# Last units of w_out by column halves over both token halves, and the first token half's transposes behind one unit more

## The chip, the cores and the metric

One Trainium2 chip, one core. The metric is the device time of the kernel in microseconds (us). The core has TensorE (matmuls), VectorE, ScalarE, GpSimd and SyncE (SP, which issues nearly all transfers here), and 16 DMA engines that bring the weights from memory.

## What is computed

A hybrid encoder layer on 256 tokens of width 1024: an RMS norm, a wide projection, a gated linear attention branch and a Hyena branch, their gated sum `merged`, the output projection `w_out`, and then a mixture of 32 experts of which each token takes 4. The part that matters here is the end of the mixer and the start of the experts:

```python
merged = jax.nn.sigmoid(g_gla) * (o_gla @ w_branch_gla) + jax.nn.sigmoid(g_hy) * (o_hy @ w_branch_hy)
h = h + merged @ w_out
hn = rms_norm(h, norm2_w)
h = h + moe_ffn(hn, router_w, router_b, w_gate_up, b_gate_up, w_down, b_down)
...
logits = ht.astype(jnp.float32) @ router_w.astype(jnp.float32) + router_b.astype(jnp.float32)
top_vals, top_idx = lax.top_k(logits, TOP_K)
```

All of it is float32. The weights of the 32 experts are about 400 MB and are read once.

## The kernel before

**The front.** Weights come in chunks of 1 MB through four front slots of the ring, two units to a chunk. Each unit is split by ScalarE and VectorE into a high and a low part ("parts"), and TensorE makes three passes per block of 128 rows. `w_out` has eight units: four units (two blocks of rows each) for each of two column halves. With the 256 tokens in two halves there are four PSUM banks, named `wo` + column half + token half: `wo00`, `wo01`, `wo10`, `wo11`. One unit for one token half is six matmuls of 128x512. Units 0 and 1 of both column halves run first for both token halves; units 2 and 3 are the last units. Step ("wo", half, a) runs both last units of one bank, twelve matmuls; ("wo_part", u) runs one of them for `wo11`, six matmuls.

**The list of stages.** `schedule()` writes out one list. TensorE, ScalarE and VectorE each walk through the whole list in order and do their own share of each stage, so the list fixes the order on each of the three engines; an engine waits on semaphores where it needs another's result. The tail of the list is on lines 263 to 265. What each step is:

- `wo`, `wo_part`: TensorE's matmuls (line 881); VectorE adds the finished bank to the residual `x` (line 1957).
- `hT` a n: four TensorE transposes of token half a, column half n of `x` (line 846); VectorE multiplies the bank by the norm's weight into `hT` (line 2005).
- `ss2` a: ScalarE's sum of squares and root of token half a (lines 1391 and 1456); `rs2`: VectorE's reciprocal (line 1972).
- `hn` a: ScalarE's high part of the normed token half (line 1460), then VectorE's low part (line 1739).
- `rl` a: the router product (TensorE, line 1123), then VectorE's logits, top-4 and mask (lines 1981 to 1989). `rank` a: the ranks of the chosen tokens (TensorE lines 1135 and 1136, VectorE lines 1993 and 1733).
- `total` 0 starts the output accumulation (line 955), `bias0` loads the biases of expert 0 (line 962). Then come the gathers (lines 947 and 939) and the experts (line 1161 gate and up, 1179 down).

**The loads.** SP issues the expert weights in a fixed order into a ring of 18 slots (and two places aside). Behind `w_out` the loads of chunks 12 to 15 each wait until a front chunk has been used (line 791): chunk 14 waits for bank `wo01`, chunk 15 for `wo11`. Later loads wait until TensorE has used the chunk that held the slot (`chunks_used`, line 807, by `uses_before`, line 169): chunk 20 waits for the first chunk of expert 0; chunks 6 and 7 lie aside and free no slot, and chunk 26, the load issued at 346.53 us, waits for chunk 8, the first of expert 1.

Of the kernel before, what the change touches and what calls it, by code (L numbers as in the profile page):

```python
# [223 lines left out]
def schedule():  # L224

    hyena = [("proj", k, 4 * half + b) for half in range(2) for k in ("hv", "hx") for b in range(4)]
    hyena += [("proj", "h0", b) for b in range(DB)]

    def tok(kind, half, units=range(4)):
        return [("tok", kind, half, u) for u in units]

    v0, v1 = tok("v", 0), tok("v", 1)
    st = [("xT", n) for n in range(4)] + v0[:1] + [("wa_parts",), ("filter", 1)] + v0[1:] + [("a_low",), ("filter", 2)]
    st += v1[:1] + [("gates", 0), ("gates", 1)] + v1[1:2] + [("gates", 2), ("gates", 3)]
    st += v1[2:3] + [("decay", 0)] + v1[3:] + [("decay", 1)]
    st += [("proj", "q", 0), ("proj", "q", 1)] + [("taps", 0, c) for c in TAP_ORDER] + [("proj", "q", 2), ("softplus",)]
    st += [("taps", 1, c) for c in TAP_ORDER] + [("proj", "q", 3), ("proj", "k", 0), ("sums", 0), ("proj", "k", 1), ("energy",)]
    st += [("proj", "k", 2), ("square", 0), ("proj", "k", 3)]  # L240
    rest = [[("energy_rest", 3 * h + i - 6)] if 2 <= h and 3 * h + i < 11 else [] for h in range(HEADS) for i in range(3)]
    for h in range(HEADS):
        st += [("scores", h)] + hyena[6 * h:6 * h + 2] + ([] if h else [("square", 1)]) + rest[3 * h]
        st += [("output", h)] + ([("sums", h + 1)] if h + 1 < HEADS else [])
        st += hyena[6 * h + 2:6 * h + 4] + rest[3 * h + 1] + hyena[6 * h + 4:6 * h + 6] + rest[3 * h + 2]
    st += [("ksum",), ("onorm",)] + [("zt", a, half) for half in range(2) for a in range(TB)]
    st += [("K", ri, half) for ri in range(2) for half in range(2)] + [("Z", half) for half in range(2)]
    r0, r1 = tok("r", 0), tok("r", 1)
    gg0, wg0, gg1 = tok("gg", 0), tok("wg", 0), tok("gg", 1)

    def Z(half, *steps):
        return [("Zmul", half, k) for k in steps]

    st += r0[:1] + Z(0, 0, 1) + r0[1:2] + Z(0, 2, 3) + r0[2:3] + Z(0, 4, 5) + r0[3:]
    st += r1[:1] + Z(0, 6) + [("silu", 0)] + r1[1:2] + Z(0, 7) + r1[2:3] + Z(1, 0) + r1[3:] + [("silu", 1), ("gated",)]
    st += gg0[:2] + [("oT", n) for n in range(4)] + gg0[2:4] + Z(1, 1)
    for u in range(4):
        st += wg0[u:u + 1] + Z(1, 2 + u) + [("zbias", u)]
    st += gg1[:1] + Z(1, 6) + gg1[1:2] + Z(1, 7) + gg1[2:]
    st += [("y", b) for b in range(DB)] + tok("wg", 1) + [("ohy_parts",)] + tok("gh", 0) + [("bias_parts",)] + tok("wh", 0)  # L260
    st += tok("gh", 1) + [("mT", 0), ("mT", 1)] + tok("wh", 1)
    st += tok("wo", 0, (0, 1)) + tok("wo", 1, (0,)) + [("mT", 2), ("mT", 3)] + tok("wo", 1, (1,))
    st += [("prepare",), ("wo", 0, 0), ("wo", 1, 0), ("ss2", 0), ("wo", 0, 1), ("hT", 0, 0), ("hT", 0, 1), ("rs2", 0), ("hn", 0)]
    st += [("wo_part", 2), ("rl", 0), ("hT", 1, 0), ("wo_part", 3), ("ss2", 1), ("total", 0), ("hT", 1, 1), ("rs2", 1)]
    st += [("rank", 0), ("rl", 1), ("bias0",), ("hn", 1), ("rank", 1)]

    def last_use(j):
        kind, nm, at, *u = UNITS[j]
        if nm == "wo" and u[0] > 1:
            return st.index(("wo_part", 3) if at else ("wo", 0, 1))  # L270
        return st.index(UNITS[j])

    for j in range(len(UNITS)):
        after = [st.index(("xT", min(j, 4) - 1)) if j else -1]
        if j // UNITS_PER_CHUNK >= FSLOTS:
            after.append(last_use((j // UNITS_PER_CHUNK - FSLOTS + 1) * UNITS_PER_CHUNK - 1))
        if j >= HI_BUFS:
            after.append(last_use(j - HI_BUFS))
        if j:
            after.append(st.index(("parts", j - 1)))  # L280
        st.insert(max(after) + 1, ("parts", j))
    return st


STAGES = schedule()
assert [s for s in STAGES if s in UNITS] == [u for u in UNITS if u[1] != "wo" or u[3] < 2]

# [1853 lines left out]
```

## Time and profile before

| | |
|---|---|
| median of 3 runs | 1248.22 us (1247.18 to 1248.77) |
| profiled run, its own time | 1248.36 us |
| span of the profiled run | 1246.6 us |
| mean granted TensorE clock | 0.998 |
| TensorE busy | 1166.2 us (94%) |
| VectorE busy | 416.2 us (33%) |
| ScalarE busy | 267.9 us (21%) |
| chain that ended last | TensorE 71%, DMA 22%, VectorE 4%, ScalarE 2% |

The span runs from the first to the last instruction; 1.8 us of the profiled run's time lie around it. Times in the rows below are from the start of the span. A busy share is a mean over stages with different limits; what the change touches lies between 304 and 320 us.

### The profile page before, as it was taken

To read this page: it belongs to the slowest core of one execution; us is meant where nothing else is said; L and a number is where in the kernel's file an instruction comes from. 1 tells how busy PE (TensorE), PEld (TensorE's weight loads), DVE (VectorE), ACT (ScalarE), POOL (GpSimd) and SP (SyncE) were. 2 spreads that over 40 slices of the span, in tenths; PEclk is the share of its full clock that TensorE was granted. 3 is DMA by queue.
4 is the path that set the end of the run, shared out by engine and by line. 5 is a ranking of instruction groups with operands and counts; after the bars stand their busy time and mean duration, and the time that the engine had idled before them with its cause. 6 is when DMAs were issued, how large, how long until landed. Compare 5 with 4: busy or idle time off the path is not lost.

```text
span 1246.6 us, 13718 instructions
## 1 busy us (share of the span) xinstructions
PE 1166.2 (94%) x5828; PEld 598.0 (48%) x5828; DVE 416.2 (33%) x702; ACT 267.9 (21%) x420; POOL 0.2 (0%) x4
## 2 busy tenths in 40 slices
PE   7999999999999999999999999988998899889986
PEld 6899968888533333343333334333433333233332
DVE  7677878756421122121212121211221121111212
ACT  6966546444200000010010001000100000001002
POOL 0000000000000000000000000000000000000000
PEclk9999999999999999999999999999999999999999
DMA  9455425698999999999999999999999999999995
GB/s 323 140 146 159 144 94 171 235 382 309 360 375 430 428 426 427 428 428 428 427 427 428 427 427 427 428 428 428 428 427 428 427 428 427 428 426 428 427 425 225
DMA packets 66941, 455.20 MB, mean 365 GB/s; under 512 B 6874, under 2 KB 23547, under 8 KB 39614
## 3 DMA queue, kind: packets, MB, share of 16 engines
q1 hardware_dynamic: 65302, 454.00, 89.1%
q8 instruction: 48, 0.79, 0.3%
q10 hardware_dynamic: 1576, 0.29, 0.1%
q14 instruction: 15, 0.12, 0.0%
HBM read 453.22 MB, written 1.05 MB: 364 GB/s over the span
## 4 chain that ended last, share of the span: by engine, by line
PE 71%; DMA 22%; DVE 4%; ACT 2%; issue 1%; SPq 0%; DVEq 0%; ACTq 0%
PE bank L1161 23%; DMA ring<-in_w_gate_up 18%; PE bank L1179 14%; PE total L881 6%; PE bank L881 4%; PE total L869 4%; PE bank L869 3%; DMA ring<-in_w_down 3%; PE bank L939 2%; PE bank L1147 2%; PE bank L1168 1%; PE total L1161 1%; ACT xn_area L1618 1%; PE bank L962 1%; PE total L1190 1%
## 5 line engine op out<-in xcount | busy, mean ns | idle before, releaser
L1161 PE MATMUL bank<-ring,hy_area 128*64 128x512 f32 x1984 | 441.8, 596 | 21.9 <-DMA ring<-in_w_gate_up 21.7
L1161 PEld LDWEIGHTS bank<-ring,hy_area 128*64 128x64 f32 x1984 | 135.6, 137 | 298.7 <-issue 251.5
L1179 PE MATMUL bank<-ring,xn_area 128*64 128x512 f32 x992 | 220.1, 595 | 20.6 <-ACT xn_area L1618 20.3
L1179 PEld LDWEIGHTS bank<-ring,xn_area 128*64 128x64 f32 x992 | 68.4, 137 | 150.6 <-issue 122.8
L2039 DVE TENSOR_SCALAR qk_area<-bank 128x512 f32<-128x512 f32 x31 | 21.5, 692 | 342.9 <-PE bank L1161 342.9
L2050 DVE SCALAR_TENSOR_TENSOR xn_area_r<-bank,tmp_area,xn_area_r 128x512 fp32r<-128x512 f32 x31 | 23.3, 751 | 307.0 <-ACT xn_area_r L1625 307.0
L1614 ACT ACTIVATE qk_area<-qk_area 128x512 f32<-128x512 f32 x32 | 20.2, 631 | 461.3 <-DVE qk_area L2039 461.3
L1747 DVE TENSOR_TENSOR front_r<-ring,slot_r 128x1024 fp32r<-128x1024 f32 x60 | 73.2, 1222 | 24.2 <-ACT slot_r L1426 24.1
L1426 ACT CAST slot_r<-ring 128x1024 fp32r<-128x1024 f32 x60 | 62.8, 1049 | 43.1 <-PE bank L881 23.2
L1625 ACT ACTIVATE xn_area_r<-bank,tmp_area 128x512 fp32r<-128x512 f32 x31 | 21.3, 687 | 229.1 <-PE bank L1179 212.0
L962 PE MATMUL bank<-tmp_area_r 128*128 128x512 f32 x124 | 36.9, 419 | 13.5 <-issue 8.5
L881 PE MATMUL total<-front_r,slot_r 128*128 128x512 f32 x112 | 43.6, 389 | 0.0
L1190 PE MATMUL total<-xn_area_r 64*128 64x512 f32 x248 | 37.2, 418 | 0.0
L1147 PE MATMUL bank<-tmp_area,tab 64*128 64x256 f32 x128 | 36.1, 402 | 0.7 <-ACT xn_area L1618 0.7
L2012 DVE TENSOR_SCALAR hy_area<-bank,colw 128x256 f32<-128x256 f32 x32 | 14.0, 478 | 66.3 <-PE bank L939 66.3
L1618 ACT COPY xn_area<-bank 128x512 f32<-128x512 f32 x31 | 18.2, 586 | 79.6 <-PE bank L1168 79.6
L962 PEld LDWEIGHTS bank<-tmp_area_r 128*128 128x128 f32 x124 | 20.9, 188 | 29.7 <-DVE qk_area L2040 15.5
L1147 PEld LDWEIGHTS bank<-tmp_area,tab 64*128 64x128 f32 x128 | 21.4, 185 | 27.9 <-issue 25.2
L1190 PEld LDWEIGHTS total<-xn_area_r 64*128 64x128 f32 x248 | 20.9, 184 | 27.9 <-issue 25.2
L881 PE MATMUL bank<-front_r,slot_r 128*128 128x512 f32 x76 | 29.6, 390 | 0.0
L1747 DVE TENSOR_TENSOR front_r<-ring,hi_late_r 128x1024 fp32r<-128x1024 f32 x20 | 24.5, 1223 | 13.7 <-ACT hi_late_r L1426 13.7
L1168 PE MATMUL bank<-tab,qk_area 128*128 128x128 f32 x128 | 22.3, 296 | 6.6 <-DVE qk_area L2045 6.6
(401 smaller groups left out, 1253.5 us busy)
## 6 DMA issues: line engine op xcount, KB each, us to landing
ring<-in_w_gate_up SPq DMA_DIRECT2D x116, 2048.0 KB, 34.6
ring<-in_w_down SPq DMA_DIRECT2D x54, 2048.0 KB, 34.9
ring<-in_w_in SPq DMA_DIRECT2D x31, 1024.0 KB, 5.6
ring<-in_w_gate_up SPq DMA_DIRECT2D x22, 1024.0 KB, 7.8
ring<-in_w_down SPq DMA_DIRECT2D x19, 1024.0 KB, 12.2
ring<-in_w_branch_gla SPq DMA_DIRECT2D x4, 1024.0 KB, 5.1
ring<-in_w_branch_hy SPq DMA_DIRECT2D x4, 1024.0 KB, 6.4
ring<-in_w_out SPq DMA_DIRECT2D x4, 1024.0 KB, 6.3
```

The costliest lines, as they stand in the source:

```text
L869: last = pe.matmul(t[:, 0:SEQ], w[:, d, :], act[:, d, :], start=(m == 0 and d == 0), stop=(m == 2 and d == DB - 1))
L881: last = pe.matmul(bank(f"{kind}{half}{a}")[:, :], act[:, d, a * P:(a + 1) * P], w[:, i, :], start=(u == 0 and i == 0 and m == 0), stop=(u ...
L939: last = pe.matmul(banks[bank_of][:, i * width:(i + 1) * width], src[:, a, d_cols(d)], moving, start=(m == 0 and a == 0), stop=(m == 1 and ...
L962: pe.matmul(gu_banks(e)[bk][:, :], b_pick[e % 2][:, bk * P:(bk + 1) * P], part, start=(m == 0), stop=(m == 1))
L1147: last = pe.matmul(banks[3][:, k * SEQ:(k + 1) * SEQ], ident[0:2 * E, k * E + e:k * E + e + 1].to_broadcast([2 * E, P]), posT_combT, start ...
L1161: last = pe.matmul(to[bk][half * CAP:(half + 1) * CAP, :], xeT[:, j, q, :], where(j, c), start=False, stop=(j == GU_CH - 1), skip_group_ch ...
L1168: last = pe.transpose(banks[3][:, c * P:(c + 1) * P], act[:, c:4 * P:4], ident)
L1179: last = pe.matmul(banks[to][half * CAP:(half + 1) * CAP, :], half_of(turned, f), where(j, c * D + half * 512), start=(f == 0), stop=(f == ...
L1190: last = pe.matmul(banks[4 + 2 * a + half], selT[r, q, a * P:(a + 1) * P], part[r, :], start=False, stop=True, skip_group_check=True)
L1426: nc.scalar.copy(unit_hi(j), unit_of(j)).then_inc(w_hi_ready, 1)
L1618: nc.scalar.copy(turned.rearrange("p c s -> p (c s)"), banks[3][:, :]).then_inc(actT_ready, 1)
L1747: nc.vector.tensor_tensor(unit_of(j, as_r["front"]), unit_of(j), unit_hi(j).bitcast(F32), ALU.subtract).then_inc(w_parts_ready, 1)
```

## The change

Two lines of the list of stages change. The steps of `wo01` move in front of `wo10`, so that both token halves of column half 0 come first and column half 1 follows. `wo_part 2` moves in front of the two transposes of token half 0, and `hT10` moves in front of `rl0`. The steps that follow keep their order.

```diff
-    st += [("prepare",), ("wo", 0, 0), ("wo", 1, 0), ("ss2", 0), ("wo", 0, 1), ("hT", 0, 0), ("hT", 0, 1), ("rs2", 0), ("hn", 0)]
-    st += [("wo_part", 2), ("rl", 0), ("hT", 1, 0), ("wo_part", 3), ("ss2", 1), ("total", 0), ("hT", 1, 1), ("rs2", 1)]
+    st += [("prepare",), ("wo", 0, 0), ("wo", 0, 1), ("wo", 1, 0), ("ss2", 0), ("wo_part", 2), ("hT", 0, 0), ("hT", 0, 1), ("rs2", 0), ("hn", 0)]
+    st += [("hT", 1, 0), ("rl", 0), ("wo_part", 3), ("ss2", 1), ("total", 0), ("hT", 1, 1), ("rs2", 1)]
     st += [("rank", 0), ("rl", 1), ("bias0",), ("hn", 1), ("rank", 1)]
```

The order on TensorE, before and after:

```
before  wo00  wo10  wo01  hT00 hT01  wo_part2  rl0   hT10  wo_part3  total0  hT11  rank0  rl1 ...
after   wo00  wo01  wo10  wo_part2  hT00 hT01  hT10  rl0   wo_part3  total0  hT11  rank0  rl1 ...
```

On VectorE the additions for `wo10` and `wo01` change places, and the product of `hT10` comes ahead of the router chain of `rl0`; on ScalarE the order stays. The PSUM banks and the places of the unit splits in the list stay.

## Rows read from the trace of the kernel before

**Rows 1.** Windows: stretch, length, engines busy (instructions), granted clock, DMA share, GB/s.
```profile
309.00:311.00 2.00, 2.00 (x14) 1.75 (x13) 0.85 (x2) 0.65 (x3) 0.00 (x0) 1.00 0.02 8
...
315.00:317.00 2.00, 1.80 (x7) 0.80 (x6) 1.82 (x7) 0.00 (x0) 0.00 (x0) 1.00 0.15 33
317.00:346.00 29.00, 28.41 (x150) 14.78 (x152) 11.40 (x35) 8.47 (x15) 0.00 (x0) 1.00 1.00 398
346.00:350.00 4.00, 3.33 (x18) 1.23 (x16) 0.95 (x3) 0.59 (x1) 0.00 (x0) 1.00 0.67 211
...
360.00:1200.00 840.00, 778.87 (x3649) 299.94 (x3645) 158.91 (x304) 67.61 (x116) 0.00 (x0) 1.00 1.01 428
```

**Rows 2.** Chain in order of time, late: start us, us, what.
```profile
830.31 39.17 DMA ring<-in_w_gate_up
```

**Rows 3.** Timeline of SP: start us, us, engine, line, operation, count.
```profile
310.14 0.33 SPq L748 DMA_DIRECT2D ring<-in_w_gate_up  x1
...
315.95 0.33 SPq L748 DMA_DIRECT2D ring<-in_w_gate_up  x1
...
346.53 5.34 SPq L748 DMA_DIRECT2D ring<-in_w_gate_up  x3
```

**Rows 4.** Timeline of TensorE, 307 to 318 us, idle before it in brackets.
```profile
307.22 0.39 PE L881 MATMUL total<-v_area_r,xn_area_r 128*128 128x512 f32 x1
...
309.95 1.03 PE L846 MATMUL total<-tab,x 128*128 128x128 f32 x8
310.74 0.48 PE L881 MATMUL bank<-tmp_area_r,xn_area_r 128*128 128x512 f32 x1
...
312.20 1.86 PE L1123 MATMUL bank<-tmp_area,hy_area 128*128 128x32 f32 x16
313.90 0.64 PE L846 MATMUL total<-tab,x 128*128 128x128 f32 x4
...
315.53 0.39 PE L881 MATMUL bank<-qk_area_r,slot_r 128*128 128x512 f32 x1
315.76 1.02 PE L955 MATMUL total<-x,tab 128*128 128x512 f32 x2
316.98 0.66 PE L846 MATMUL total<-tab,x 128*128 128x128 f32 x4 [0.20 <-DVE x L1957]
```

**Rows 5.** Timeline of VectorE, 310 to 317 us.
```profile
310.15 0.69 DVE L1957 TENSOR_TENSOR x<-total,x 128x512 f32<-128x512 f32 x1 [2.03 <-PE total L881]
310.75 1.28 DVE L2005 TENSOR_TENSOR hy_area<-total,colw 128x512 f32<-128x512 f32 x2
311.95 0.15 DVE L1972 RECIPROCAL small<-small 128x1 f32<-128x1 f32 x1
313.32 1.28 DVE L1739 SCALAR_TENSOR_TENSOR gla_area_r<-x,small,v_area_r 128x1024 fp32r<-128x1024 f32 x1 [1.22 <-ACT v_area_r L1460]
314.52 0.24 DVE L1981 SCALAR_TENSOR_TENSOR tmp_area<-bank,small,tmp_area 128x32 f32<-128x32 f32 x1
...
315.65 0.68 DVE L2005 TENSOR_TENSOR hy_area<-total,colw 128x512 f32<-128x512 f32 x1
316.25 0.68 DVE L1957 TENSOR_TENSOR x<-bank,x 128x512 f32<-128x512 f32 x1
```

**Rows 6.** Timeline of ScalarE, the sum of squares of token half 0.
```profile
308.21 1.06 ACT L1391 ACTIVATE gla_area<-x 128x1024 f32<-128x1024 f32 x1 [3.90 <-DVE x L1957]
...
309.39 0.30 ACT L1456 ACTIVATE small<-small 128x1 f32<-128x1 f32 x1
```

**Rows 7.** Waits of TensorE, 317 to 347 us: total us, times, longest.
```profile
PE bank L1135 <- DVE tmp_area L1989: 0.3, 1, 0.3
PE bank L947 <- DVE qk_area_r L1733: 0.3, 1, 0.3
```

**Rows 8.** Timeline of TensorE behind a longer wait, 369 us.
```profile
369.59 1.16 PE L962 MATMUL bank<-tmp_area_r 128*128 128x512 f32 x4 [1.44 <-issue]
370.68 3.65 PE L1161 MATMUL bank<-ring,hy_area 128*64 128x512 f32 x16
```

## The prediction

> **What bounds the kernel now.** I read the page's busy slices first, then the chain of waits in order of time, then the timelines of the three engines around the changed steps, then the DMA share in windows. From 360 us to 1200 us the DMA engines are never free, 428 GB/s at a share of 1.01, while the loads wait only for ring slots [rows 1]; the late chain runs through loads that need 39.17 us from issue to landing [rows 2]. So the end of the kernel is the moment from which the DMA engines stay full, plus a fixed number of bytes. That moment lies just behind 346 us. From 317 to 346 the engines are full too (1.00, 398 GB/s), then comes a hole: 211 GB/s in 346 to 350 [rows 1]. The hole ends with the load issued at 346.53 [rows 3], which SP holds (line 807) until TensorE has used the chunk in its ring slot, the first chunk of expert 1. TensorE therefore sets the start of the full stretch, and what counts is when it gets there. What moves TensorE at 317 us moves the end; what only moves a transfer before 317 us doesn't, unless it closes the hole at 346.
>
> In the changed stretch TensorE has work without a gap until 316.8; then `hT11` begins 0.20 us late, released by VectorE's addition into `x` on line 1957 [rows 4]. VectorE is the engine to watch. From 310.15 it does one thing after another: the addition for `wo01`, the two products of `hT00` and `hT01`, the reciprocal, the low part of `hn` (after ScalarE's high part), the router chain of token half 0, the product of `hT10`, and only then the addition for `wo11` at 316.25 [rows 5]. The product of that addition is what `hT11` transposes, and behind it stand the second router product, its top-4 mask, rank and first gather: nothing in that row can be done without it.
>
> **The change part by part.** Nothing is added or removed: TensorE does the same 48 `w_out` matmuls (three groups of twelve, two parts of six), the same transposes, the same router products. Two things move.
>
> (1) `wo01` runs second and `wo10` third. Twelve matmuls take 309.95 - 307.22 = 2.73 us [rows 4]. So bank `wo01` is complete at about 307.4 instead of 310.1 and `wo10` at 310.1 instead of 307.4. Weight parts: `wo10` needs the last two units, which are now needed 2.73 us later; TensorE shows no wait for them before, so this frees nothing. ScalarE's `ss2` of token half 0 needs both `wo00` and `wo10`, so it moves from 308.21 to about 310.94 and ends, after the 1.48 us from 308.21 to 309.39 + 0.30 [rows 6], at 312.42. SP's queue: the load of chunk 14 waits for `wo01`; it goes out at about 307.4 instead of 310.14 [rows 3]. The next load, at 315.95, waits for `wo11`, whose place is the same, so SP then only stands there longer.
>
> (2) The six matmuls of `wo_part 2` come ahead of `hT00` and `hT01`, and `hT10` ahead of `rl0`. In the new order the six begin at 309.95, where the transposes began. Six of them cost half of 2.73, 1.36 us, so the transposes begin at 311.31. Four transposes are complete 0.64 to 0.66 us after their start (the two groups of four, [rows 4]), at 311.97, and VectorE takes the first product at about 312.00. Before it took it at 310.75 [rows 5], held up by its own addition. **Delay 1.25 us.** The cover that the six matmuls lend to the addition of `wo10` (310.15 to 310.84) was not needed: TensorE had no wait there.
>
> From this product to the addition for `wo11` VectorE needs 316.25 - 310.75 = 5.50 us [rows 5]. The list of work in it is the same; `hT10` and the router chain only swap places. Could a wait inside become shorter? The reciprocal comes straight behind the products (311.95, now 313.20) and its input is there at 312.42, so it does not wait; the low part of `hn` stands 1.22 us idle for ScalarE's high part [rows 5], as before. Could one become longer? `rl0` starts when the product of `hT00` is done: 312.00 + 0.68 = 312.7, some 0.2 us behind the end of the transposes of `hT10`, and takes 1.86 us [rows 4], to 314.6; VectorE reaches it only at 316.4 (the low part at 313.32 + 1.25 = 314.57, the product of `hT10` 1.20 behind it as the router chain was before, and 0.60 for that product, the step from 315.65 to 316.25 [rows 5]). So neither. The addition for `wo11` moves to 317.50, although TensorE has that bank ready at 316.1 (315.53 + 0.39 and the 0.2 us before `rl0`) [rows 4]. `hT11` starts 0.73 us after the addition's start (316.25 to 316.98), at 318.23: TensorE stands idle for about 1.3 us where it stood 0.20. Queued behind `hT11` on TensorE are the rank, the second router product, `bias0`, the gathers and all of expert 0; VectorE, ScalarE and SP wait for those. Between `hT11` and 347 TensorE stood still only for two waits of 0.3 us, both for VectorE's work on that same row of steps [rows 7], so there is no slack to take the delay up.
>
> Bounds of the 1.25. Least: the first four transposes count as done when the next instruction starts, 0.79 / 2 = 0.40 us (eight from 309.95 to 310.74, [rows 4]): 309.95 + 1.36 + 0.40 - 310.75 = 0.96. Most: the six matmuls take the 1.46 us that they took between 310.74 and 312.20 [rows 4], VectorE sees the product only after all eight transposes (1.03), and the 0.2 us in front of `rl0` comes on top: 1.46 + 1.03 + 309.95 - 310.75 + 0.21 = 1.90. A gain is excluded: VectorE cannot begin the product before six more matmuls are through. I take 1.25, from the rows of just such groups of four.
>
> Then the DMA. With TensorE 1.25 us later the load of 346.53 goes out at 347.8. The loads before it stay queued: 317 to 346 is full, so their end at about 346 stays. The hole grows by 1.25 us and everything behind it shifts. The early load of chunk 14 fills the hole of 309 to 311 (8 GB/s), but the engines run empty again at 315 to 317 (33 GB/s) in either order [rows 1], so it is worth nothing at the end. Sum: + 1.25 us. On the profiled run that is 1248.36 + 1.25 = 1249.6, on the median of the three runs 1248.22 + 1.25 = **1249.5 us**; the profiled run lies 0.14 us above that median, within the spread of the runs.
>
> A rule that speaks the other way: the Trainium skill, Perfetto Trace Analysis, section Optimization Strategy, says to look for the gaps on the most contended engine and make what they wait for start sooner. Here that is the DMA, and the load of chunk 14 does start sooner; by that rule alone it is a gain, which is the second rival. The windows at 315 to 317 are what I hold against it.
>
> **The rivals.**
> *Absorbed.* TensorE's 1.25 us vanish because the loads at 346 are not held by TensorE, or because the DMA has a slack that I don't see: 1248.2. For it: TensorE has slack late in the run. Against it: what is full late is the DMA, and the hole at 346 precedes it.
> *The early load pays.* If the order of loads, not TensorE, sets the start of the full stretch, closing the hole of 309 to 311 (2.0 us at 8 GB/s) is a gain of 2.0: 1246.2. Against it is the second hole. That the change doesn't do what it says here (SP held by something else) gives the first rival's time.
> *Slower: the clock.* The new wait of TensorE, about 1.3 us with thin work around it, makes the granted clock fall to the lower level (1.2 of 2.4 GHz). Price: the work between `hT11` at 316.98 and 324 takes twice as long, some 6 us beside the delay, 1249.5 + 6 = 1255.5. It decides from the point where the granted clock after the wait is below 1.00. Against it: the trace has a wait of 1.44 us before 369.59, and sixteen expert matmuls behind it take 3.65 us [rows 8] in a stretch with a granted clock of 1.00 [rows 1]. The Trainium skill, Perfetto Trace Analysis, section Matmul Optimizations, says that TensorE's power follows its use and matmuls should come back to back; by that the time would be this rival's, but no gap of this size shows it here.
>
> **How the numbers follow.** Forecast 0.71, absorbed 0.15, early load 0.09, clock 0.05. The forecast's own bounds are 1248.22 + 0.96 = 1249.2 and 1248.22 + 1.90 = 1250.1. The three runs reach 1.04 us from their median, which I allow on both sides of the forecast's upper bound and the absorbed time: 1248.2 - 1.0 = 1247.2 to 1250.1 + 1.1 = 1251.2. That leaves out the early load and the clock, 14 in 100, and a little of the tails. About 0.2% (2.5 us) is what a measurement of this kernel can tell from no change. Forecast and absorbed lie within it, but for the upper tail (above 1250.7, some 0.09); the early load at 1246.2 straddles the lower bound (0.05 of its 0.09 falls beyond, with the tail of the absorbed case); the clock is beyond. Faster 0.06, same 0.80, slower 0.14.
>
> **What would show it.** After: the first product of `hT00` on VectorE at about 312.0; the addition for `wo11` starting some 1.3 us later than before while its bank is long ready; `hT11` on TensorE at about 318.2 with a wait of 1.2 to 1.5 us released by line 1957; chunk 14's load out at about 307.4; the load of 346.53 at about 347.8, with the hole before it longer. The prediction is wrong if `hT11` is late but that load is not, if that load is late but the full stretch is not, or if VectorE's 5.50 us change their length.

## The result, and the profile after

The changed kernel takes 1250.62 us (median of 20 executions, 1248.19 to 1251.92), the kernel before 1248.75 (20 executions on the same chips). The ratio is 1.0015, 95% interval 1.0009 to 1.0021: slower by 1.1 to 2.6 us. Three executions in the comparisons below took far longer than all others (2006.97, 3110.26 and 4187.98 us, one each of `units_first`, `late_at_631` and `col_order`), and the medians, ratios and counts leave them out. The profiled execution of the changed kernel took 1249.99 us with a span of 1248.2. Its trace runs 0.22 us late already ahead of the change, as VectorE's first addition into `x` shows, which has the same place in both; I take this off below.

Timeline of VectorE, kernel before, then kernel after:

```profile
305.33 0.69 DVE L1957 TENSOR_TENSOR x<-total,x 128x512 f32<-128x512 f32 x1
```
```profile
305.55 0.68 DVE L1957 TENSOR_TENSOR x<-total,x 128x512 f32<-128x512 f32 x1
...
310.39 0.69 DVE L1957 TENSOR_TENSOR x<-bank,x 128x512 f32<-128x512 f32 x1 [2.03 <-PE bank L881]
312.19 1.29 DVE L2005 TENSOR_TENSOR hy_area<-total,colw 128x512 f32<-128x512 f32 x2 [1.11 <-PE total L846]
313.40 0.15 DVE L1972 RECIPROCAL small<-small 128x1 f32<-128x1 f32 x1
314.77 1.28 DVE L1739 SCALAR_TENSOR_TENSOR gla_area_r<-x,small,v_area_r 128x1024 fp32r<-128x1024 f32 x1 [1.22 <-ACT v_area_r L1460]
315.97 0.68 DVE L2005 TENSOR_TENSOR hy_area<-total,colw 128x512 f32<-128x512 f32 x1
316.57 0.24 DVE L1981 SCALAR_TENSOR_TENSOR tmp_area<-bank,small,tmp_area 128x32 f32<-128x32 f32 x1
...
317.70 0.68 DVE L1957 TENSOR_TENSOR x<-bank,x 128x512 f32<-128x512 f32 x1
```

VectorE now stands idle for 1.11 us in front of the first product of `hT00`, where before it came straight from its addition [rows 5]. From 312.19 to the addition for `wo11` it takes 5.51 us; before it was 5.50.

Timeline of TensorE, kernel after:

```profile
311.56 1.47 PE L846 MATMUL total<-tab,x 128*128 128x128 f32 x12
313.03 1.94 PE L1123 MATMUL bank<-tmp_area,hy_area 128*128 128x32 f32 x16
...
316.05 0.39 PE L881 MATMUL bank<-qk_area_r,slot_r 128*128 128x512 f32 x1
316.28 1.02 PE L955 MATMUL total<-x,tab 128*128 128x512 f32 x2
318.44 0.66 PE L846 MATMUL total<-tab,x 128*128 128x128 f32 x4 [1.14 <-DVE x L1957]
```

`hT11` starts at 318.44 instead of 316.98 [rows 4] and waits 1.14 us instead of 0.20, for the addition on line 1957, while its bank was complete at 316.4.

Timeline of SP, and windows (columns as in rows 1), kernel after:

```profile
307.67 0.33 SPq L748 DMA_DIRECT2D ring<-in_w_gate_up  x1
...
347.98 10.49 SPq L748 DMA_DIRECT2D ring<-in_w_gate_up  x6
```
```profile
309.00:311.00 2.00, 2.00 (x10) 1.65 (x10) 0.61 (x1) 0.00 (x0) 0.00 (x0) 1.00 1.01 365
315.00:317.00 2.00, 2.00 (x8) 1.21 (x7) 1.97 (x4) 0.00 (x0) 0.00 (x0) 1.00 0.00 0
317.00:346.00 29.00, 27.30 (x143) 14.21 (x142) 11.28 (x40) 8.13 (x15) 0.00 (x0) 1.00 0.99 392
320.00:326.00 6.00, 5.43 (x38) 4.32 (x39) 5.18 (x22) 3.90 (x7) 0.00 (x0) 1.00 1.01 427
346.00:350.00 4.00, 4.00 (x20) 1.47 (x20) 2.33 (x5) 0.35 (x1) 0.00 (x0) 1.00 0.46 137
...
360.00:1200.00 840.00, 779.05 (x3650) 299.96 (x3648) 158.64 (x306) 66.98 (x115) 0.00 (x0) 1.00 1.01 428
```

Window of 313 to 314, kernel before, then kernel after:

```profile
313.00:314.00 1.00, 1.00 (x11) 1.00 (x11) 0.68 (x1) 0.29 (x1) 0.00 (x0) 1.00 0.96 401
```
```profile
313.00:314.00 1.00, 1.00 (x10) 1.00 (x9) 0.55 (x2) 0.41 (x1) 0.00 (x0) 1.00 0.08 33
```

The early load of chunk 14 fills the hole of 309 to 311 (365 GB/s instead of 8), and what was loaded early is missing behind it: 33 GB/s instead of 401 in 313 to 314. The second hole, at 315 to 317, stays (0 instead of 33 GB/s; it is as empty in `hT10_early`, where nothing is loaded early). The load that ended the hole at 346 went out at 347.98 instead of 346.53 [rows 3], and 346 to 350 carry 137 GB/s instead of 211 [rows 1]. Behind it the DMA engines are full as before. The last expert load landed at 1225.40 us instead of 1223.97, by the chain of waits of both traces: 1.43 us, or 1.21 without the 0.22. Chain in order of time, kernel before, then kernel after (start, us, what):

```profile
1184.83 39.14 DMA ring<-in_w_down
```
```profile
1186.25 39.15 DMA ring<-in_w_down
```

So the trace of this execution shows the forecast's 1.25 us. The 20 executions show 1.87 in the median. The experiments had to tell which part of the change makes the 1.25, and where the rest comes from.

### The profile page after: what moved, and what is told of

The parts are those of the page before. It is cut to its first block, busy times and chain, and to the rows that moved or that the text cites. A ratio compares the mean times of both kernels' runs of the same rounds, so it can differ in the third digit from the quotient of the medians.

```text
span 1248.2 us, 13718 instructions
## 1 busy us (share of the span) xinstructions
PE 1166.5 (93%) x5828; PEld 598.7 (48%) x5828; DVE 416.2 (33%) x702; ACT 267.8 (21%) x420; POOL 0.2 (0%) x4
## 4 chain that ended last, share of the span: by engine, by line
PE 70%; DMA 22%; DVE 4%; ACT 2%; issue 2%; DVEq 0%; ACTq 0%
PE bank L1161 23%; DMA ring<-in_w_gate_up 18%; PE bank L1179 14%; PE total L881 6%; PE bank L881 4%; PE total L869 4%; PE bank L869 3%; DMA ring<-in_w_down 3%; PE bank L939 2%; PE bank L1147 2%; PE bank L1168 1%; PE total L1161 1%; ACT xn_area L1618 1%; PE bank L962 1%; PE total L1190 1%
```

## The experiments

Differences are against executions of the kernel before on the same chip. "Low clock" counts executions with a mean granted TensorE clock of 0.995 or less; of 98 executions of the kernel before in these comparisons none was so low.

| kernel | median, before | ratio (95% interval) | load of 346.53 out at | low clock |
|---|---|---|---|---|
| `col_order` | 1248.96, 1248.79 | 1.0004 (0.9995 to 1.0013) | 347.02 | 0 of 10 |
| `part_ahead` | 1249.70, 1248.79 | 1.0010 (1.0001 to 1.0019) | 350.03 | 0 of 11 |
| `swap_only` | 1248.35, 1248.79 | 0.9997 (0.9988 to 1.0006) | 346.65 | 0 of 11 |
| `add_ahead` | 1251.69, 1248.79 | 1.0021 (1.0012 to 1.0030) | 348.04 | 6 of 11 |
| `late_at_316` | 1251.89, 1248.34 | 1.0034 (1.0021 to 1.0047) | 350.50 | 0 of 5 |
| `late_at_631` | 1246.69, 1248.34 | 0.9988 (0.9980 to 0.9997) | 346.53 | 0 of 11 |
| `units_first` | 1249.26, 1248.34 | 1.0013 (1.0004 to 1.0022) | | 4 of 11 |
| `units_first_again` | 1250.23, 1248.32 | 1.0013 (1.0004 to 1.0022) | 348.74 | 5 of 11 |
| `change_again` | 1249.50, 1248.32 | 1.0008 (0.9999 to 1.0017) | 349.52 | 3 of 11 |
| `wait_filled` | 1249.45, 1248.32 | 1.0007 (0.9998 to 1.0016) | 347.58 | 0 of 11 |
| `hT10_early` | 1248.48, 1248.45 | 1.0000 (0.9991 to 1.0009) | 346.43 | 0 of 11 |

### One part of the change at a time

`col_order`: the column order alone.

```diff
-    ("prepare",), ("wo", 0, 0), ("wo", 1, 0), ("ss2", 0), ("wo", 0, 1), ("hT", 0, 0), ("hT", 0, 1), ...
+    ("prepare",), ("wo", 0, 0), ("wo", 0, 1), ("wo", 1, 0), ("ss2", 0), ("hT", 0, 0), ("hT", 0, 1), ...
```

> Only the column order is changed: wo01 runs ahead of wo10, wo_part 2 stays behind hT00 and hT01. Theory (VectorE's row of work from the first product of hT00 to the addition for wo11 sets when TensorE can go on): the first product still starts at about 310.8 us, the second one about 0.2 us later because hT01 waits for the addition of wo10, and the reciprocal waits for ScalarE's root, which ends at about 312.4 instead of 309.7, so the low part of hn and all behind it come some 0.5 us later: hT11 at about 317.5 instead of 316.98, total +0.3 to +0.6 us. Rival (the earlier load of chunk 14 pays): -2.0 us. Rival (the column order is the main part of the loss): +1.2 us or more.

TensorE waits in front of `hT01` for the addition of `wo10`, and `hT11` starts at 317.49. Timeline of TensorE, `col_order`:

```profile
310.89 0.66 PE L846 MATMUL total<-tab,x 128*128 128x128 f32 x4 [0.35 <-DVE x L1957]
...
317.49 0.66 PE L846 MATMUL total<-tab,x 128*128 128x128 f32 x4
```

The load goes out 0.49 us late, as expected; the total (0.2 us in the median) agrees with that, though its interval also holds zero. An early load of chunk 14 worth 2 us is excluded, since that load is early here too.

`part_ahead`: `wo_part 2` ahead of `hT00` and `hT01` alone.

```diff
-    ..., ("wo", 0, 1), ("hT", 0, 0), ("hT", 0, 1), ("rs2", 0), ("hn", 0), ("wo_part", 2), ("rl", 0), ...
+    ..., ("wo", 0, 1), ("wo_part", 2), ("hT", 0, 0), ("hT", 0, 1), ("rs2", 0), ("hn", 0), ("rl", 0), ...
```

> Only wo_part 2 is moved ahead of hT00 and hT01; columns in the old order, hT10 behind rl0 as before. Theory: the first product starts six matmuls later, at about 312.0 us, VectorE's row of 5.5 us is the same, hT11 at about 318.2 with a wait of about 1.2 us, total +1.25 us, the whole of the change's loss. Rival (the column order or the swap of hT10 and rl0 makes the loss): 0 to +0.3 us.

`hT11` starts at 318.40, 1.42 us later than before (1.27 without the 0.15 us that this trace runs late at VectorE's first addition); the transposes of `hT00` start at 311.52 in this trace and at 311.56 in that of the change, so the whole delay of the change is here. The expected wait of 1.2 us is two waits, 0.44 us in front of `rl0` and 0.75 in front of `hT11`. The total is 0.9 us up in the median (0.1 to 2.4 by the ratio), where 1.25 was expected. But the load at 346.53 went out at 350.03, 2.05 us behind even the change. Timeline of TensorE in the kernel before, then timeline of TensorE and a window of `part_ahead`:

```profile
319.40 1.17 PE L962 MATMUL total<-tmp_area_r 128*128 128x512 f32 x4
```
```profile
318.40 0.66 PE L846 MATMUL total<-tab,x 128*128 128x128 f32 x4 [0.75 <-DVE x L1957]
...
321.12 2.05 PE L962 MATMUL total<-tmp_area_r 128*128 128x512 f32 x4
```
```profile
320.00:326.00 6.00, 6.00 (x27) 5.49 (x27) 4.30 (x18) 3.13 (x6) 0.00 (x0) 0.54 1.00 416
```

The four matmuls of `bias0` take 2.05 us where they took 1.17 in the trace before, and the granted clock of the stretch is 0.54: the lower of the two levels, 1.2 of 2.4 GHz, for most of it. This is the rival to which I had given 5 in 100. It was there in this profiled execution (1251.72 us), not in the median of the runs (1249.70).

`swap_only`: `hT10` ahead of `rl0` alone.

```diff
-    [("wo_part", 2), ("rl", 0), ("hT", 1, 0), ("wo_part", 3), ...
+    [("wo_part", 2), ("hT", 1, 0), ("rl", 0), ("wo_part", 3), ...
```

> Only hT10 and rl0 change places. Theory: VectorE's row of work keeps its length and its start, hT11 stays at about 317.0, total 0.0 (-0.2 to +0.2) us. Rival (the product of hT10 ahead of the router chain delays what follows): +0.7 us.

`hT11` starts at 317.10 behind transposes that started 0.11 us later than before, the load goes out at 346.65: nothing changed, as expected.

### Is it the place of the addition, or the sum of VectorE's work

`add_ahead`: the changed kernel; in VectorE's walk through the list the addition comes ahead of the product of `hT10`.

```diff
-            for stage in STAGES:
+            mine = [s for s in STAGES if s != ("wo_part", 3)]
+            mine.insert(mine.index(("hT", 1, 0)), ("wo_part", 3))
+            for stage in mine:
```

> The changed kernel, but VectorE takes the addition for wo11 ahead of the product of hT10 and of the router chain of token half 0; TensorE and ScalarE keep the order of the change. Theory (it is the sum of VectorE's work, not the place of the addition): hT11 goes out at about 317.3 without a wait, but rank0 behind it now waits for the mask of rl0, which is finished at about 318.9, so the wait of about 1.1 us moves from hT11 to rank0 and the total stays that of the change, +1.0 to +1.9 us against before. Rival (the place of the addition is the cause): back to the time of before, within 0.3 us.

Timeline of TensorE, `add_ahead`:

```profile
317.17 0.66 PE L846 MATMUL total<-tab,x 128*128 128x128 f32 x4
318.89 0.41 PE L1136 MATMUL bank<-tmp_area,tab 128*128 128x32 f32 x2 [1.06 <-DVE tmp_area L1991]
```

`hT11` waits for nothing and the same wait stands one step later, in front of the rank, for the mask of the first token half. The load goes out at 348.04, as in the change (347.98). So the sum of VectorE's work counts and not the place of this addition. The total is 2.6 us up by the ratio, more than the 1.0 to 1.9 expected; six of the eleven executions have a low clock (mean 1251.9 us, the other five 1250.4).

### Where the end is set

`late_at_316` and `late_at_631`: TensorE held back at two places by work that changes nothing in what the kernel returns.

```diff
-                    start_total(*at)
+                    for _ in range(6):
+                        start_total(*at)
```

> The kernel before with TensorE held back by about 5.3 us: the start of the output accumulation (total 0) is run six times instead of once, the result is the same. It stands ahead of the hole in the transfers at 346 us. Theory (TensorE sets when the DMA engines become full for good): the load of 346.53 goes out about 5.1 us later and the total is +5.1 us (4.6 to 5.6). Rival (a delay of TensorE is taken up later, since the DMA is the bound): +0 to +1 us.

```diff
             def spread_rows(e):
+                if e == 11:
+                    for _ in range(10):
+                        pe.matmul(banks[3][:, 0:SEQ], ident[0:2 * E, e:e + 1].to_broadcast([2 * E, P]), posT_combT, start=True, stop=True)
```

> The kernel before with TensorE held back by about the same 5.3 us, at 631 us, behind the down projection of expert 10: ten more broadcasts of the row tables into a bank that is written over. There the DMA engines are full and loads land some 30 us after their issue. Theory (from 347 us on only the DMA counts): total 0.0 us (-0.3 to +0.3), the chunks land as before. Rival (TensorE bounds the kernel until about 830 us, as the chain of waits puts it): +5.3 us.

Timelines of TensorE, `late_at_316`, then `late_at_631`:

```profile
315.87 5.31 PE L955 MATMUL total<-x,tab 128*128 128x512 f32 x12
321.02 0.60 PE L846 MATMUL total<-tab,x 128*128 128x128 f32 x4
```
```profile
631.32 4.58 PE L1148 MATMUL bank<-tmp_area,tab 64*128 64x256 f32 x20
635.74 1.02 PE L1150 MATMUL bank<-tmp_area,tab 64*128 64x256 f32 x4
```

The early delay is smaller than I meant: all six starts take 5.31 us, the five added ones some 4.3, and `hT11` is 4.04 us late. The load at 346.53 is 3.97 us late, the total 3.55 in the median (2.6 to 5.9 by the ratio). Delay in front of the hole and time at the end go together. So it is in all eleven traces of changed orders and delays: the last expert load lands between 0.58 us earlier and 0.29 us later than the delay of the load of 346.53 says. The late delay is 4.3 us too, and nothing of it appears at the end; instead the kernel is 1.6 us faster (0.4 to 2.5). That TensorE bounds the kernel at 631 us is excluded. In the traces 0.5 us of it lie ahead of the last expert load (landed at 1223.46 instead of 1223.97, no more than the scatter just named), and the rest behind TensorE's last work, in the last two stores of the output, which land 2.5 us after their issue instead of 3.6. But those are at 2.5 in some traces of other kernels (`swap_only`, `late_at_316`, `change_again`) and at 3.6 to 3.8 in the rest, without regard to the edit. Why the stores differ, and why all 11 executions of this kernel are so fast, stays open.

### The granted clock

`change_again` is the changed kernel once more. `wait_filled` is the changed kernel with its wait filled by work:

```diff
-                    start_total(*at)
+                    for _ in range(2):
+                        start_total(*at)
```

> The changed kernel once more, on the same chip as the filled wait. Theory of the clock: two groups of executions, with mean clocks of 0.997 and 0.998 at about +1.2 us against before, and of 0.994 to 0.996 at about +2.8 us. Rival: one group, times that don't go with the clock.

> The changed kernel with its wait of 1.14 us in front of hT11 filled: the start of the output accumulation (total 0) is run twice, with the same result, so TensorE works for some 0.9 to 1.0 us more of that wait. VectorE's row of work is untouched, so hT11 stays at about 318.4 us. Theory of the clock (the wait lets the granted clock fall in part of the executions, which makes the changed kernel's mean clock 0.994 to 0.996 in 9 of 20 of them and costs those about 2 us): no execution below 0.996, and the median falls to +0.9 to +1.4 us against before, less than the change's +1.9. Rival (the falls of the clock have nothing to do with the wait, or the loss is VectorE's row alone): the same spread of clocks and the same median as the change.

Timeline of TensorE and windows, `change_again`:

```profile
311.01 1.48 PE L846 MATMUL total<-tab,x 128*128 128x128 f32 x12
...
317.89 0.66 PE L846 MATMUL total<-tab,x 128*128 128x128 f32 x4 [1.13 <-DVE x L1957]
...
320.56 2.05 PE L962 MATMUL total<-tmp_area_r 128*128 128x512 f32 x4
```
```profile
316.00:320.00 4.00, 2.87 (x22) 2.11 (x20) 2.92 (x13) 1.82 (x4) 0.00 (x0) 1.00 0.75 254
320.00:326.00 6.00, 6.00 (x26) 5.48 (x26) 4.32 (x19) 3.32 (x7) 0.00 (x0) 0.50 1.01 423
326.00:330.00 4.00, 4.00 (x19) 1.80 (x20) 1.01 (x4) 0.21 (x1) 0.00 (x0) 0.89 1.00 410
```

The same program, the same wait of 1.13 us, but here the clock is at the lower level from 320 to 326. From the first transpose to the load out it takes 349.52 - 311.01 = 38.51 us; in the first trace of the change 347.98 - 311.56 = 36.42. The fall costs 2.1 us. A low clock comes in a part of the executions: of 31 of the changed kernel, 10 have a low clock and a mean of 1251.4 us, the other 21 a mean of 1249.4. Ten times 2.0 over 31 is 0.65 us, about what the median of the first comparison has above the 1.25.

But the two comparisons differ: the median of the second lies only 1.18 us above the kernel before. There the expectation of two groups came true in part: the five executions at 0.994 to 0.996 have a mean 2.3 us above that of the kernel before (expected 2.8), the six at 0.998 and 0.999 lie at its level (1248.4 and 1248.5 us), where +1.2 was expected; in the first comparison the eleven at 0.997 and 0.998 lie 1.1 us above. The 1.1 us by which the last stores differ from trace to trace is as large as this gap; whether it makes it is not shown.

The count of low clocks is a lower bound: this profiled execution has a mean clock of 0.996 and the fall all the same. At 0.996 stand 4 of the 31 executions, but also 11 of the 98 of the kernel before, 1.0 us above its others in the mean, so that a fall in some of those is not excluded.

The same with the wait filled, `wait_filled`, timeline of TensorE and window:

```profile
315.88 1.88 PE L955 MATMUL total<-x,tab 128*128 128x512 f32 x4
318.04 0.66 PE L846 MATMUL total<-tab,x 128*128 128x128 f32 x4 [0.28 <-DVE x L1958]
```
```profile
320.00:326.00 6.00, 5.41 (x36) 4.03 (x37) 5.21 (x21) 3.67 (x7) 0.00 (x0) 1.00 1.02 423
```

`hT11` is no earlier (its distance to the first transpose, 6.89 us, is that of the change, 6.88). None of 11 executions is below 0.996, against 10 of 31 without the filling. The median is + 1.1 us, in the forecast's place. But `change_again` came out at the same median on this chip, so the gain in time by the filling is not shown. At a rate of 10 in 31, no low clock in 11 executions would come by chance about once in 70 sets; on this chip alone it is 0 of 11 against 3 of 11, which proves little. That the filling keeps the clock up is likely, not proven, and whether it does so because a wait is gone or because wide work has come in is not told apart.

### A better order

`units_first`, run a second time as `units_first_again` for its trace; both start from the kernel before.

```diff
+    ..., ("hT", 0, 0), ("hT", 0, 1), ("rs2", 0), ("hT", 1, 0), ("hn", 0)]
+    st += [("wo_part", 2), ("wo_part", 3), ("ss2", 1), ("total", 0), ("hT", 1, 1), ("rs2", 1)]
+    st += [("rl", 0), ("rl", 1), ("rank", 0), ("bias0",), ("hn", 1), ("rank", 1)]
```

> A try at a better order from the theory, starting from the kernel before: hT10 directly behind hT00 and hT01, then both parts of wo11, then hT11, and only then both router products. VectorE's idle time while ScalarE makes the high part of hn takes the product of hT10, and the addition for wo11 does not stand behind the router chain. Theory: hT11 at about 315.3 us instead of 316.98, the last gather of the first group 0.4 to 0.8 us earlier, total -0.4 to -0.8 us against before. Rival (TensorE's own sum of work is the bound there): 0.0 us.

> The reordered kernel of units_first once more, to see its trace: hT10 behind hT01, both parts of wo11 next, then hT11, then both router products. Theory from VectorE's row: hT11 at about 315.3 us and the gathers 0.4 to 0.8 us earlier, so executions with a mean clock of 0.997 and above at -0.3 to -0.8 us against before, and the loss of the earlier run lies in executions with a lower clock, behind waits of TensorE of 0.5 us and more in front of rank0 or rank1. Rival: the gathers are no earlier than before, and the loss is in the order itself, at every clock.

Timeline of TensorE and windows, `units_first_again`:

```profile
315.21 0.66 PE L846 MATMUL total<-tab,x 128*128 128x128 f32 x4
315.71 3.66 PE L1123 MATMUL bank<-tmp_area,hy_area 128*128 128x32 f32 x32
```
```profile
316.00:320.00 4.00, 4.00 (x36) 3.92 (x36) 2.36 (x12) 3.54 (x7) 0.00 (x0) 1.00 0.94 373
320.00:326.00 6.00, 6.00 (x25) 4.97 (x25) 4.63 (x19) 1.16 (x3) 0.00 (x0) 0.50 1.00 422
```

`hT11` is where I wanted it, at 315.21 and without a wait. Yet the kernel is slower. VectorE now waits for the router products (0.70 and 0.57 us in its timeline) and its second mask is done at 320.62 instead of 320.82, so the gain shrinks to 0.2 us. And the clock falls here too, in a stretch in which TensorE never stood still: 4.00 of 4.00 us busy, but with transposes and 32 router matmuls of 32 columns. I had expected waits of 0.5 us in front of the fall; there were none. Nor did the gain show at a high clock: the executions at 0.997 and above, five in the first run and two in the second, are 0.2 and 0.4 us above the kernel before in the mean, where 0.3 to 0.8 less was expected. So few of them don't tell whether the order itself costs something too.

`hT10_early` keeps the wide matmuls between the router products:

```diff
-    ..., ("hT", 0, 0), ("hT", 0, 1), ("rs2", 0), ("hn", 0)]
-    st += [("wo_part", 2), ("rl", 0), ("hT", 1, 0), ("wo_part", 3), ...
+    ..., ("hT", 0, 0), ("hT", 0, 1), ("rs2", 0), ("hT", 1, 0), ("hn", 0)]
+    st += [("wo_part", 2), ("rl", 0), ("wo_part", 3), ...
```

> From the kernel before: only hT10 is moved, directly behind hT00 and hT01, and its product on VectorE behind the reciprocal, into the 1.22 us in which VectorE waits for ScalarE's high part of hn. Both router products keep wide matmuls between them. Theory of VectorE's row: the row gets 0.6 us shorter, the addition for wo11 then waits for its bank (about 315.95 us instead of 316.25), hT11 goes out at about 316.8 without a wait, the load of 346.53 some 0.1 to 0.3 us earlier, total -0.1 to -0.3 us, which the runs can hardly tell from nothing; the spread of clocks is that of before. Rival (the clock falls because less wide work stands in front of the router products): executions at 0.996 and below as often as in the change, +0.5 us or more.

Timeline of VectorE, `hT10_early`:

```profile
312.03 0.67 DVE L2005 TENSOR_TENSOR hy_area<-total,colw 128x512 f32<-128x512 f32 x1
313.33 1.28 DVE L1739 SCALAR_TENSOR_TENSOR gla_area_r<-x,small,v_area_r 128x1024 fp32r<-128x1024 f32 x1 [0.63 <-ACT v_area_r L1460]
...
316.13 0.69 DVE L1957 TENSOR_TENSOR x<-bank,x 128x512 f32<-128x512 f32 x1 [0.23 <-PE bank L881]
```

The product fits into VectorE's idle time, and the addition now waits for TensorE. `hT11` is at 316.88, the load at 346.43, both 0.10 us earlier than before. That is all that this order gives, and the runs can't tell it from nothing. None of its 11 executions has a mean clock of 0.996 or less (14 of 31 of the changed kernel), so the rival of this run is out.

## Why the prediction was right, and where it was not

- **The time.** 1250.62 instead of 1249.5. Of the 1.12 between them 0.53 is the kernel before, 1248.22 in the three runs that I started from and 1248.75 in twenty; the rest is the change, + 1.87 instead of + 1.25. That the time lies in the range says little, since the range holds "no change" as well; the wait and the late load below say more.
- **The bound.** Right. A delay in front of 346 us comes out at the end (`late_at_316`), one behind it does not (`late_at_631`).
- **The first product, 312.00.** 312.19, or 311.97 without the trace's 0.22.
- **VectorE's 5.50 us.** 5.51. That swapping `hT10` and `rl0` costs nothing was right (`swap_only`), and `part_ahead` shows that the six matmuls ahead of the transposes make the delay. I had the column order at nothing; alone it costs 0.5 us at the load (`col_order`), which in the change lies behind the six matmuls.
- **`hT11` at 318.23.** 318.44, or 318.22. The wait was 1.14 instead of 1.3, since `rl0` ended later than I had worked out and the bank was complete at 316.4.
- **The load at 347.8.** 347.98, or 347.76: the whole 1.25 us (1.23) came through, as forecast.
- **The early load.** Worth nothing, by the second hole, as I had held. The rule of the Trainium skill (Perfetto Trace Analysis, section Optimization Strategy) to look for the gaps on the most contended engine named the right engine; the gap was the wrong one.
- **The clock.** This is the step that was mis-sized. I took the wait of 1.44 us before 369.59, behind which the clock stayed at 1.00 [rows 8], as evidence against a fall. That wait stands between wide expert matmuls; the new one stands in a stretch of transposes and narrow router products, and there the clock was low in 10 of 31 executions. I had also priced it wrongly, at 6 us by doubling all the work from `hT11` on; the fall costs 2.1. In `change_again` the clock was still at 1.00 in the first 2 us behind `hT11`, the work behind that took less than twice as long (`bias0` 2.05 us instead of 1.17), and the two waits of 0.3 us for VectorE [rows 7] were used up. And I made it a case that holds or doesn't; it holds in a part of the executions, so it belonged into the forecast as a mean. With a third of 2.1 on top the forecast would have been + 1.9 and not + 1.25; measured was + 1.87 in the first comparison and + 1.18 in the second, so this sum, made afterwards, fits one of them only.

The Trainium skill, Perfetto Trace Analysis, section Matmul Optimizations, asks for matmuls in back-to-back batches because TensorE's power follows its use. `change_again` agrees (0.50 behind a wait of 1.13 us), the first trace of the change does not (1.00 behind 1.14). `units_first_again` goes further than that sentence: TensorE was back to back, and the clock fell.

What stays open: why the changed kernel loses its clock in some executions and not in others, whether the wait or the narrow work around it is the cause, and why `late_at_631` is faster.

## What to carry to other kernels

A step put in front of another engine's first operation delays that engine's whole row of work, even if TensorE itself has no gap: look for the engine that is busy without a break, and ask when its first operation starts. Then find the last moment at which the transfers run empty; here a delay of TensorE ahead of it counted fully, and an earlier load ahead of another hole counted nothing. A stretch of short waits and narrow work can cost more than the waits are long, by the clock, and one trace may not show it: look at the mean clocks of many executions.

## What I had not expected of the hardware

The granted clock fell to 0.50 for some 6 us without any long wait: behind 1.13 us of waiting among transposes and narrow matmuls, and in `units_first_again` behind none at all (TensorE busy 4.00 of 4.00 us). Identical programs differ in it: the two traces of the changed kernel, 1.00 and 0.50 in the stretch from 320 to 326 us, are 2.1 us apart from the first transpose to the load behind the hole.
